# Later transposes and values in the layers' attention, and half of the differential heads' products on GpSimd

## The chip, the cores and the metric

The kernel runs on one core of a Trainium2 chip. The metric is the device time of one execution in microseconds (us), here the median of three runs. The engines are named as in the profile: PE (TensorE's matrix multiplies; PEld its weight loads), DVE (VectorE), ACT (ScalarE), POOL (GpSimd) and SP (which issues the DMAs).

## The reference, cut to what matters

The program is one transformer block with latent and sparse attention, followed by a second block of two layers. The change touches only the attention of these two layers. There, 16 heads of width 64 on 512 tokens are of three kinds: four differential heads, four block heads and eight dilated heads. Cut to the attention of a layer:

```python
# differential head: two score maps on half the width, one set of values
p = softmax(where(causal, q[c] @ k[c].T * 32 ** -0.5, NEG))   # c = 0, 1
a = p[0] - lam * p[1]
o_a = rms_norm(a @ v, g_head) * (1.0 - lam_init)
# block head and dilated head: one score map each, with their own masks
o = softmax(where(mask, q @ k.T * 64 ** -0.5, NEG)) @ v
mix = concat(o_a, o_b, o_c); x = x + mix @ w_out
```

The queries come in four blocks of 128, and a causal block j needs only the first 128 (j + 1) keys.

## The kernel before

All is in fp32. Large projections split weights and activations into a high and a low part (fp32r) and multiply three times; POOL makes the two parts of most weight slabs (`w_hi<-raw,zero_c` and `w_lo<-raw,w_hi`).

The attention of a layer is written as a list of units (`two_units`, class `Weave`). A unit has two score maps of one query block: two heads side by side ("pair"), or the two maps of one differential head ("diff"). The first 28 units are eight triples of one pair and two diffs (half 0 and half 1), with 512, 128, 384, 256 keys and the same again, and four "turn" units (numbers 6, 13, 17 and 24) that transpose operands for later. Sixteen dilated pairs follow in the same rhythm of key counts, and one "out" unit among them transposes the finished differential heads.

Every engine runs the list in its own order, in steps; step t does one part for unit t and others for units that lie a lag behind:

- PE: scores of unit t (L1845), values of unit t-5 (L1880 for pairs, L1886 for diffs), transposes of the probabilities of unit t-3 (L1862).
- DVE: mask of unit t with its row minimum (L3808), then `weigh` of unit t-1: for a pair the reciprocals of the two sums (L3817); for half 1 of a differential head the ratio of the sums (L3823, L3824) and after it the combined probabilities of both halves, `two = two * r + one` (L3829, once for each half). It also copies the second transposed tile of dilated pairs (L3837) and takes finished groups out (L3795, L3849, L3850).
- ACT: copy of the transposed tiles of unit t-3 (L2865), then the exponentials of unit t with their sums (L2857).
- POOL (`scale_pairs`): for each pair, in the order of units, waits for the reciprocals, scales both maps (L1140), and then makes one eighth of the next two weight slabs (L1104, a drain, L1108), for the eight pairs of the first 28 units; the dilated pairs have none left.

Diffs are not touched by POOL before the change. When all four differential heads are done, POOL squares them (L1123), DVE sums (L3865), ACT takes roots (L2881), DVE inverts, and POOL multiplies by gain and scale (L1127, L1132). Steps for these are fixed by numbers that count from DIFF_AT.

Buffers: four masked maps, eight probability maps, two PSUM banks for transposes, four transposed tiles.

Of the kernel before, what the change touches and what calls it, by code (L numbers as in the profile page):

```python
# [222 lines left out]
def build(nc, xT_d, slabs_d, ada_d, c_d, cols_d, rows_d, consts_d, strips_d, pos_d, cpos_d,  # L223
# [5 lines left out]
    with ctx:  # L229
# [475 lines left out]
        dilated_jobs = [job(dilated_q[h // 2], T2a[:, h // 2, :], lambda kb, h=h: z2[:, 5, kb, 64 * h:64 * h + 64],  # L705
                            None, strip2[:]) for h in range(8)]

        LAG_T, LAG_V, LAG_OUT = 3, 5, 6
        W_MASKED, W_PROBS, W_TURNED = 4, 8, 4

        class Unit:

# [15 lines left out]
        class Weave:  # L728


            def __init__(self, units):
                self.units = units
                scores = tiles = values = pairs = joins = on_act = on_dve = diffs = 0
                turned_a = 0
                self.tiles_of, self.value_of = [], []
                ends = {}
                for t, u in enumerate(units):
                    u.t, u.bank = t, 2 * (t % 2)
                    u.score, u.tile = scores, tiles
                    if u.kind == "turn":  # L740
                        turned_a += sum(len(two_turns[n][2]) for n in u.items)
                        u.turned_a = turned_a
                    if not u.jobs:
                        continue
                    scores += 2
                    values += 1
                    u.value = values
# [12 lines left out]
                for u in ends.values():  # L760
                    u.last = True
                out_order = sorted(ends, key=lambda g: ends[g].t)
                self.released = {g.index: n + 1 for n, g in enumerate(out_order)}
                self.high, self.low = {}, {}
                for t in range(len(units) + LAG_OUT):
                    if t < len(units) and units[t].kind == "out":
                        for i in units[t].items:
                            self.high[i], self.low[i] = len(self.high) + 1, len(self.low) + 1
                    for found, lag in ((self.high, LAG_V), (self.low, LAG_OUT)):
                        u = units[t - lag] if 0 <= t - lag < len(units) else None  # L770
                        if u is not None and u.last and u.group.block is not None:
# [12 lines left out]
                self.scores, self.tiles, self.values, self.pairs, self.joins = scores, tiles, values, pairs, joins  # L784
                self.on_act, self.on_dve, self.groups = on_act, on_dve, len(ends)

            def at(self, t):
# [3 lines left out]

        def sum_at(u, c):
            if u.kind == "pair":
                return 20 + 2 * (u.pair % 4) + c
            return 16 + u.join % 4 if c else 8 * (u.group.index // 2 % 2) + 4 * u.half + u.j

        def o_high(i):
# [1 line left out]
            return o_hi[:, (i + 4) % KD, :]  # L799

        def pair_inv(u):
            a = 224 + 2 * (u.pair % 4)
            return stats[:, a:a + 2]

        def w_masked(i, n):
            return ring_2[:, i % W_MASKED, 0:n]

        def w_probs(i, n):
            return ring_2[:, W_MASKED + i % W_PROBS, 0:n]

        def w_turned(v, n):
            return ring_2[:, W_MASKED + W_PROBS + v % W_TURNED, 0:n]

        HEAD = 8

# [57 lines left out]
            units.insert(DIFF_TURN, Unit("out", items=(6, 7)))  # L873
            return Weave(units)

        DILATED_AT = 28
        DIFF_AT = DILATED_AT - 1 + LAG_OUT
        DIFF_SQ, DIFF_SUM, DIFF_GAIN, DIFF_ROOT, DIFF_SCALE, DIFF_TURN = (DIFF_AT + n for n in (1, 2, 3, 3, 4, 8))

        def turn_split(src, hi, lo, n, gains=None):  # L880
            return [(lambda tt, i=i: src(tt, i), hi[:, i, :], lo[:, i, :], gains[i] if gains else None)
# [99 lines left out]
        def _(pool):  # L981
# [132 lines left out]
            def scale_pairs(n, plan, layer):  # L1114

                pieces = itertools.chain(pieces_of(n), pieces_of(n + 1))
                released = plan.groups * layer + len(nsa_jobs + mla_jobs) + plan.released[3]
                heads = O2[:].rearrange("p t (h d) -> p t h d", d=HD)
                shape = list(heads.shape)
                for u in plan.units:  # L1120
                    if u.t == DIFF_SQ:
                        pool.wait_ge(out_used, released)
                        nc.gpsimd.tensor_tensor(sq_2[:], O2[:].rearrange("p t f -> p (t f)"),  # L1123
                                                O2[:].rearrange("p t f -> p (t f)"), ALU.mult).then_inc(diff_pool, 1)
                    if u.t == DIFF_GAIN:
                        pool.wait_ge(diff_pool, 2 * layer + 1)
                        nc.gpsimd.tensor_tensor(heads, heads, row("diff", layer * HD, HD).unsqueeze(1).unsqueeze(1)  # L1127
                                                .to_broadcast(shape), ALU.mult)
                    if u.t == DIFF_SCALE + 1:
                        pool.drain()  # L1130
                        pool.wait_ge(diff_dve, 2 * layer + 2)
                        nc.gpsimd.tensor_tensor(heads, heads, stats[:, 0:16].rearrange("p (t h) -> p t h", t=TT)  # L1132
                                                .unsqueeze(3).to_broadcast(shape), ALU.mult).then_inc(diff_pool, 1)
                    if u.kind != "pair":
                        continue
                    pool.wait_ge(inverted, plan.pairs * layer + u.pair + 1)
                    inv = pair_inv(u)
# [150 lines left out]
        def _(pe):  # L1288
# [522 lines left out]
            def weave(plan, two_turned, layer, tail):  # L1811
# [37 lines left out]
                def turns(u):  # L1849
# [2 lines left out]
                        pe.wait_ge(last_taken_dve, layer + 1)  # L1852
                    for c in (0, 1) if u.kind == "pair" else (1,):
                        v = u.tile + (c if u.kind == "pair" else 0)
                        if u.kind == "diff":
                            pe.wait_ge(combined, at_.pair + u.join + 1)
                        elif c == 0:
                            pe.wait_ge(scaled_probs, at_.scaled + u.pair + 1)
                        if v >= PT_BANKS:
                            copied_before(v - PT_BANKS)  # L1860
                        for b in range(u.nb):
# [40 lines left out]
            def woven(plan):  # L1902
                at_.tile += plan.scores
                at_.value += plan.tiles
                at_.pvs += plan.values
                at_.pair += plan.joins
                at_.scaled += plan.pairs
# [998 lines left out]
        def _(dve):  # L2906
# [774 lines left out]
            for layer in range(LAYERS):  # L3681
# [131 lines left out]
                def weigh(u):  # L3813
# [5 lines left out]
                    if u.half == 0:  # L3819
# [4 lines left out]
                    then(V.scalar_tensor_tensor(out=r, in0=r, scalar=lam_c, in1=SUMS[:, a - 4:a + 1:4], op0=ALU.mult,  # L3824
                                                op1=ALU.mult))
                    for half in (0, 1):
                        score = plan.at(u.t - 1 + half).score
                        one, two = (w_probs(score + c, 128 * u.nb) for c in (0, 1))
                        V.scalar_tensor_tensor(out=two, in0=two, scalar=r[:, half:half + 1], in1=one, op0=ALU.mult,  # L3829
                                               op1=ALU.add).then_inc(combined, 1)  # L3830

                def copy(u):
                    v = u.tile + 1
# [22 lines left out]
                for t in range(len(plan.units) + LAG_OUT):  # L3856
                    u = plan.at(t)
                    if u is not None:
                        front(u)
                    u = plan.at(t - 1)  # L3860
                    if u is not None and u.jobs:
                        weigh(u)
                    if t == DIFF_SUM:
# [154 lines left out]
```

## Time and profile before

| | |
|---|---|
| median of three runs | 2188.46 us (2188.44 to 2190.65) |
| the profiled execution | 2188.03 us, of which the span is 2185.9 us |
| PE busy, whole span | 2122.7 us (97%) |
| attention of layer 0 / layer 1 in the span | from 1025 to about 1122 us / from 1666 to about 1763 us |
| PE's idle time ahead of the transposes there | 8.5 us / 8.8 us |

PE is the engine that is busy nearly all the time, so a stretch gets shorter only where PE waits or has less to do. A row of the timeline gives start, length, engine, line, operation, what was written from what, and how many instructions are merged in it; in brackets stands the idle time of that engine just ahead of the row and who ended it. PE's rows overlap by a few tenths of a microsecond, so distances are taken from start to start.

### The profile page before, as it was taken

How to read it: one execution, taken by the hardware profiler on the slowest of the kernel's cores; microseconds unless marked ns; L12 is line 12 of the kernel's file. 1: busy time of each engine (PE TensorE's matmuls, PEld its weight loads, DVE VectorE, ACT ScalarE, POOL GpSimd, SP SyncE). 2: the span in 40 equal slices, each digit the busy share in tenths (PEclk: the TensorE clock that was granted, in tenths of full speed). 3: DMA queues.
4: the chain of work that ended last, by engine and by line, in shares of the span. 5: the costliest groups of instructions: out<-in, count | busy, mean ns of one | idle time of the engine just before them, and what ended most of it. 6: DMA issues, size and time to landing. Idle time of an engine off the chain costs nothing.

```text
span 2185.9 us, 33061 instructions
## 1 busy us (share of the span) xinstructions
PE 2122.7 (97%) x12329; PEld 1788.0 (82%) x12329; DVE 1480.3 (68%) x2224; ACT 940.1 (43%) x1875; POOL 1280.7 (59%) x720
## 2 busy tenths in 40 slices
PE   6999999999999999999999999999999999999997
PEld 4788888787899988898667898888897677888886
DVE  6834877554666592897736676677996627777676
ACT  3254663112556510544744555412545725455312
POOL 5756404766477677753556644577653657454675
PEclk9999999999999999999999999999999999999998
DMA  8322103422133233221102222322321112223221
GB/s 321 154 84 97 55 25 114 175 79 94 60 115 109 105 139 135 97 97 59 39 21 77 97 97 97 116 96 78 110 84 41 39 39 97 95 80 116 97 97 58
DMA packets 32776, 206.78 MB, mean 95 GB/s; under 512 B 4080, under 2 KB 4336, under 8 KB 11632
## 3 DMA queue, kind: packets, MB, share of 16 engines
q1 hardware_dynamic: 32192, 200.27, 25.2%
q10 hardware_dynamic: 432, 4.46, 0.5%
q8 instruction: 99, 1.62, 0.3%
q14 instruction: 53, 0.43, 0.1%
HBM read 202.61 MB, written 2.10 MB: 94 GB/s over the span
## 4 chain that ended last, share of the span: by engine, by line
PE 82%; DVE 7%; issue 4%; POOL 2%; ACT 2%; DMA 2%; DVEq 1%; POOLq 1%; SPq 0%; ACTq 0%
PE PS L1293 18%; PE PS L1295 17%; PE PS L1294 17%; PE PS L1548 3%; PE PS L1549 3%; PE PS L1550 3%; PE PS L1624 2%; PE PS L1626 2%; PE PS L1625 2%; PE PS L1772 2%; PE PS L1784 2%; PE PS L1845 2%; PE PS L1862 2%; PE PS L1880 1%; PE PS L1798 1%
## 5 line engine op out<-in xcount | busy, mean ns | idle before, releaser
L997 POOL TENSOR_TENSOR w_hi<-raw,zero_c 128x512 fp32r<-128x512 f32 (+1 forms) x131 | 266.3, 2052 | 317.0 <-PE PS L1295 315.6
L1001 POOL TENSOR_TENSOR w_lo<-raw,w_hi 128x512 fp32r<-128x512 f32 (+1 forms) x131 | 347.4, 2671 | 5.5
L1293 PE MATMUL PS<-b_hi,w_hi 128*128 128x512 f32 x512 | 203.1, 397 | 0.9 <-POOL w_lo L1272 0.9
L1295 PE MATMUL PS<-b_hi,w_lo 128*128 128x512 f32 x512 | 203.0, 396 | 0.0
L1294 PE MATMUL PS<-b_lo,w_hi 128*128 128x512 f32 x512 | 203.0, 396 | 0.0
L3620 DVE TENSOR_TENSOR b_lo<-a_all,b_hi 128x512 fp32r<-128x512 f32 x44 | 162.6, 3733 | 49.3 <-ACT b_hi L2739 49.3
L1293 PE MATMUL PS<-f_hi,w_hi 128*128 128x512 f32 x448 | 177.6, 396 | 0.7 <-DVE f_lo L2921 0.7
L1295 PE MATMUL PS<-f_hi,w_lo 128*128 128x512 f32 x448 | 177.6, 396 | 0.0
L1294 PE MATMUL PS<-f_lo,w_hi 128*128 128x512 f32 x448 | 177.6, 396 | 0.0
L1140 POOL TENSOR_TENSOR ring<-ring,stats 128x512 f32<-128x512 f32 (+3 forms) x96 | 66.7, 720 | 119.1 <-DVE stats L3817 119.1
L1020 POOL TENSOR_TENSOR w_lo<-raw,w_hi 128x512 fp32r<-128x512 f32 x48 | 70.9, 1477 | 91.3 <-ACT w_hi L2731 91.3
L1293 PEld LDWEIGHTS PS<-b_hi,w_hi 128*128 128x128 f32 x512 | 96.4, 188 | 24.6 <-POOL w_lo L1272 1.1
L1295 PEld LDWEIGHTS PS<-b_hi,w_lo 128*128 128x128 f32 x512 | 96.4, 188 | 23.5
L1294 PEld LDWEIGHTS PS<-b_lo,w_hi 128*128 128x128 f32 x512 | 96.4, 188 | 23.5
L1295 PEld LDWEIGHTS PS<-f_hi,w_lo 128*128 128x128 f32 x448 | 84.4, 188 | 20.5
L1293 PEld LDWEIGHTS PS<-f_hi,w_hi 128*128 128x128 f32 x448 | 84.4, 188 | 20.1 <-issue 1.0
L1294 PEld LDWEIGHTS PS<-f_lo,w_hi 128*128 128x128 f32 x448 | 84.4, 188 | 19.1
L2739 ACT ACTIVATE b_hi<-a_all 128x512 fp32r<-128x512 f32 x44 | 25.3, 624 | 171.4 <-PE PS L1295 171.4
L1009 POOL TENSOR_TENSOR w_lo<-raw,w_hi 128x2048 fp32r<-128x2048 f32 (+1 forms) x18 | 59.1, 3295 | 62.2 <-ACT w_hi L2591 62.2
L1154 POOL TENSOR_TENSOR w_lo<-raw,w_hi 128x512 fp32r<-128x512 f32 x54 | 71.3, 1321 | 38.8 <-ACT w_hi L2629 38.8
L2857 ACT ACTIVATE ring<-ring,negmax 128x512 f32<-128x512 f32 (+3 forms) x160 | 87.8, 553 | 11.8 <-DVE negmax L3808 11.7
L3582 DVE SCALAR_TENSOR_TENSOR aux<-PS,cols,aux 128x511 f32<-128x511 f32 (+1 forms) x112 | 81.0, 741 | 14.7 <-ACT aux L2711 13.5
(588 smaller groups left out, 6826.2 us busy)
## 6 DMA issues: line engine op xcount, KB each, us to landing
raw<-slabs_dram SPq DMA_DIRECT2D x161, 1024.0 KB, 4.8
aux<-ada_dram SPq DMA_DIRECT2D x18, 512.0 KB, 5.6
ada_first<-ada_dram SPq DMA_DIRECT2D x11, 512.0 KB, 13.9
cmpw<-cmpw_dram ACTq DMA_DIRECT2D x2, 2048.0 KB, 12.9
ada_late<-ada_dram SPq DMA_DIRECT2D x8, 512.0 KB, 3.2
ada_last<-ada_dram SPq DMA_DIRECT2D x8, 512.0 KB, 5.7
xT<-xT_dram SPq DMA_DIRECT2D x1, 2048.0 KB, 9.2
out_dram<-t SPq DMA_DIRECT2D x4, 512.0 KB, 3.2
```

Source lines behind the costliest of these rows:

```text
L997: high = nc.gpsimd.tensor_tensor(w_hi[:, slot, c], raw[:, slot, c], zero[:, 0:c.stop - c.start], ALU.add)
L1001: low = nc.gpsimd.tensor_tensor(w_lo[:, slot, c], raw[:, slot, c], w_hi[:, slot, c].bitcast(f32), ALU.subtract)
L1020: return nc.gpsimd.tensor_tensor(pair_ring(w_lo, ct, n, what), pair_operand(ct, n, what), pair_ring(w_hi, ct, n, what).bitcast(f32), ALU.s ...
L1140: last = nc.gpsimd.tensor_tensor(p, p, inv[:, c:c + 1].to_broadcast([P, 128 * u.nb]), ALU.mult)
L1154: nc.gpsimd.tensor_tensor(ring_slot(w_lo, j), operand(j), ring_slot(w_hi, j).bitcast(f32), ALU.subtract).then_inc(slab_split if name == "A ...
L1293: nc.tensor.matmul(out, a_hi_, b_hi_, start=start, stop=False)
L1294: nc.tensor.matmul(out, a_hi_, b_lo_, start=False, stop=False)
L1295: return nc.tensor.matmul(out, a_lo_, b_hi_, start=False, stop=stop)
L1548: nc.tensor.matmul(out, wh[:, k, :], xh, start=first, stop=False, skip_group_check=True)
L2857: A(w_probs(i, 128 * u.nb), w_masked(i, 128 * u.nb), ACT.Exp, scale=-1.0, bias=negmax[:, i % 8:i % 8 + 1], accum_out=SUMS[:, a:a + 1]).the ...
L3582: V.scalar_tensor_tensor(out=t[:, sh:], in0=src[:, 0:SEQ - sh], scalar=cols[:, w:w + 1], in1=t[:, sh:], op0=ALU.mult, op1=ALU.add)
L3620: V.tensor_tensor(b_lo[:, f, :], a_all[:, f, :], b_hi[:, f, :].bitcast(f32), ALU.subtract).then_inc(b_low_ready, 1)
```

## The change

PE's transposes come four units behind the scores (three before), the values six (five), the outputs seven (six). DVE weighs unit t-2 in its step t (t-1 before), behind the mask of unit t. Of each differential head pair DVE now combines half 0 only; half 1 is combined by POOL in two instructions, a product with the ratio and a sum, with a drain between them. POOL takes half 1 in the order of units, so behind the pair of its triple and that pair's piece of weights. Ten probability maps are kept instead of eight (two lie in another tile), and the rings of sums and reciprocals grow from four to six. The steps of the differential norm move by up to three.

```diff
-        LAG_T, LAG_V, LAG_OUT = 3, 5, 6
-        W_MASKED, W_PROBS, W_TURNED = 4, 8, 4
+        LAG_T, LAG_V, LAG_OUT = 4, 6, 7
+        W_MASKED, W_PROBS, W_TURNED, W_SPARE = 4, 10, 4, 8
...
-        DIFF_SQ, DIFF_SUM, DIFF_GAIN, DIFF_ROOT, DIFF_SCALE, DIFF_TURN = (DIFF_AT + n for n in (1, 2, 3, 3, 4, 8))
+        DIFF_SQ, DIFF_SUM, DIFF_GAIN, DIFF_ROOT, DIFF_SCALE, DIFF_TURN = (DIFF_AT + n for n in (1, 3, 2, 4, 5, 8))
...
-                    if u.t == DIFF_SCALE + 1:
+                    if u.t == DIFF_SCALE - 1:
...
-                    if u.kind != "pair":
+                    if not u.jobs or u.kind == "diff" and u.half == 0:
                         continue
-                    pool.wait_ge(inverted, plan.pairs * layer + u.pair + 1)
+                    pool.wait_ge(inverted, plan.weighed * layer + u.weighed + 1)
+                    if u.kind == "diff":
+                        one, two = (w_probs(u.score + c, 128 * u.nb) for c in (0, 1))
+                        b = u.join % 4
+                        nc.gpsimd.tensor_tensor(two, two, ratio[:, b:b + 1].to_broadcast([P, 128 * u.nb]), ALU.mult)
+                        pool.drain()
+                        nc.gpsimd.tensor_tensor(two, two, one, ALU.add).then_inc(scaled_probs, 1)
+                        continue
...
-                        if u.kind == "diff":
-                            pe.wait_ge(combined, at_.pair + u.join + 1)
-                        elif c == 0:
-                            pe.wait_ge(scaled_probs, at_.scaled + u.pair + 1)
+                        if u.kind == "diff" and u.half == 0:
+                            pe.wait_ge(combined, at_.pair + u.join // 2 + 1)
+                        elif u.kind == "diff" or c == 0:
+                            pe.wait_ge(scaled_probs, at_.scaled + u.weighed + 1)
...
-                    for half in (0, 1):
-                        score = plan.at(u.t - 1 + half).score
-                        one, two = (w_probs(score + c, 128 * u.nb) for c in (0, 1))
-                        V.scalar_tensor_tensor(out=two, in0=two, scalar=r[:, half:half + 1], in1=one, op0=ALU.mult,
-                                               op1=ALU.add).then_inc(combined, 1)
+                    dve.drain().then_inc(inverted, 1)
+                    u = plan.at(u.t - 1)
+                    b = 16 + u.join % 4
+                    one, two = (w_probs(u.score + c, 128 * u.nb) for c in (0, 1))
+                    V.scalar_tensor_tensor(out=two, in0=two, scalar=ratio[:, b - 16:b - 15], in1=one, op0=ALU.mult,
+                                           op1=ALU.add).then_inc(combined, 1)
...
-                    u = plan.at(t - 1)
+                    u = plan.at(t - 2)
                     if u is not None and u.jobs:
                         weigh(u)
```

On POOL, at the start of a layer's attention, the order before is two scalings of a pair (ring is the tile of masked maps, probabilities and transposed tiles; stats holds reciprocals and ratios), then a piece of weights:

```order
L1140 TENSOR_TENSOR ring_133<-ring_133,stats 128x512 x2
L1104 TENSOR_TENSOR w_hi<-raw,zero_c 128x512
L1108 TENSOR_TENSOR w_lo<-raw,w_hi 128x512
L1140 TENSOR_TENSOR ring_133<-ring_133,stats 128x128 x2
L1104 TENSOR_TENSOR w_hi<-raw,zero_c 128x512
L1108 TENSOR_TENSOR w_lo<-raw,w_hi 128x512
```

Now, at the same place on POOL, with the new lines L1145 and L1147 for half 1 of a differential head:

```order
L1152 TENSOR_TENSOR ring_133<-ring_133,stats 128x512 x2
L1109 TENSOR_TENSOR w_hi<-raw,zero_c 128x512
L1113 TENSOR_TENSOR w_lo<-raw,w_hi 128x512
L1145 TENSOR_TENSOR ring_133<-ring_133,stats 128x512
L1147 TENSOR_TENSOR ring_133<-ring_133 128x512
L1152 TENSOR_TENSOR ring_133<-ring_133,stats 128x128 x2
L1109 TENSOR_TENSOR w_hi<-raw,zero_c 128x512
L1113 TENSOR_TENSOR w_lo<-raw,w_hi 128x512
L1145 TENSOR_TENSOR ring_133<-ring_133,stats 128x128
L1147 TENSOR_TENSOR ring_133<-ring_133 128x128
```

So two instructions stand behind each piece of weights, and the next pair stands behind them.

On PE, at the same start (aux and T hold the operands of the scores, consts the identity for transposes, z the values), the order before is:

```order
L1845 MATMUL PS<-aux,z_129 128x512 x2
L1845 MATMUL PS<-aux,T_131 128x512 x4
L1845 MATMUL PS<-aux,z_129 128x128 x2
L1862 MATMUL PS<-consts,ring_133 128x128 x8
L1845 MATMUL PS<-aux,T_131 128x128 x2
L1862 MATMUL PS<-consts,ring_133 128x128 x4
L1845 MATMUL PS<-aux,T_131 128x128 x2
L1880 MATMUL PS<-ring_133,z_129 64x128 x8
L1862 MATMUL PS<-consts,ring_133 128x128 x4
L1840 MATMUL PS<-consts,z_129 128x128 x8
```

Now, on PE at the same place:

```order
L1857 MATMUL PS<-aux,z_129 128x512 x2
L1857 MATMUL PS<-aux,T_131 128x512 x4
L1857 MATMUL PS<-aux,z_129 128x128 x2
L1857 MATMUL PS<-aux,T_131 128x128 x2
L1874 MATMUL PS<-consts,ring_133 128x128 x8
L1857 MATMUL PS<-aux,T_131 128x128 x2
L1874 MATMUL PS<-consts,ring_133 128x128 x4
L1852 MATMUL PS<-consts,z_129 128x128 x8
L1892 MATMUL PS<-ring_133,z_129 64x128 x8
L1874 MATMUL PS<-consts,ring_133 128x128 x4
```

The scores of one more diff (128 keys) stand ahead of the first transposes, and the turn unit (L1840, now L1852) ahead of the third.

## Rows read from the trace of the kernel before

**Rows 1.** The page: busy time and share of each engine over the span.

```profile
PE 2122.7 (97%) x12329; PEld 1788.0 (82%) x12329; DVE 1480.3 (68%) x2224; ACT 940.1 (43%) x1875; POOL 1280.7 (59%) x720
```

**Rows 2.** Stretch of layer 0's first 28 units: busy time by engine, PEclk, DMA.

```profile
1025.00:1078.00 53.00, 48.93 (x332) 34.01 (x332) 37.78 (x136) 41.22 (x127) 27.15 (x30) 1.00 0.06 21
```

**Rows 3.** PE's waits in layer 0's attention: us in total, times, longest.

```profile
PE PS L1862 <- DVE ring L3829: 3.1, 4, 0.9
PE PS L1862 <- DVE ring L3837: 2.9, 3, 1.4
PE PS L1862 <- POOL ring L1140: 1.3, 1, 1.3
PE PS L1862 <- ACT ring L2865: 1.2, 2, 0.9
```

**Rows 4.** Layer 1's attention, PE's transposes: busy, mean ns, idle before, releasers.

```profile
L1862 PE MATMUL PS<-consts,ring 128*128 128x128 f32 x156 | 25.5, 283 | 8.8 <-DVE ring L3829 3.5 <-DVE ring L3837 2.9 <-POOL ring L1140 1.2
```

**Rows 5.** Timeline of POOL just behind layer 0's attention.

```profile
1134.56 3.60 POOL L997 TENSOR_TENSOR w_hi<-raw,zero_c 128x2048 fp32r<-128x2048 f32 x1 [12.83 <-PE PS L1295]
```

**Rows 6.** Groups of DVE in layer 0's attention with waits on ACT and POOL.

```profile
L3823 DVE RECIPROCAL stats<-rowsum 128x2 f32<-128x2 f32 x8 | 1.3, 164 | 7.1 <-ACT ring L2857 7.1
L3865 DVE TENSOR_REDUCE stats<-sq 128x16 f32<-128x1024 f32 x1 | 1.2, 1220 | 1.6 <-POOL sq L1123 1.6
```

**Rows 7.** Timeline of POOL in layer 0's attention: scalings of pairs, a piece of weights.

```profile
1029.54 2.04 POOL L1140 TENSOR_TENSOR ring<-ring,stats 128x512 f32<-128x512 f32 x2 [26.68 <-DVE stats L3817]
1031.54 1.04 POOL L1104 TENSOR_TENSOR w_hi<-raw,zero_c 128x512 fp32r<-128x512 f32 x1
1032.73 1.83 POOL L1108 TENSOR_TENSOR w_lo<-raw,w_hi 128x512 fp32r<-128x512 f32 x1
...
1042.18 1.61 POOL L1140 TENSOR_TENSOR ring<-ring,stats 128x384 f32<-128x384 f32 x2 [3.34 <-DVE stats L3817]
...
1044.93 1.27 POOL L1108 TENSOR_TENSOR w_lo<-raw,w_hi 128x512 fp32r<-128x512 f32 x1
```

**Rows 8.** Groups of POOL with two different full inputs, over the whole span.

```profile
L1020 POOL TENSOR_TENSOR w_lo<-raw,w_hi 128x512 fp32r<-128x512 f32 x48 | 70.9, 1477 | 91.3 <-ACT w_hi L2731 91.3
...
L1194 POOL TENSOR_TENSOR q_m<-m_rope 128x512 f32<-128x512 f32 x1 | 1.3, 1277 | 0.1
```

**Rows 9.** Timeline of DVE in layer 0's attention: ratios and combined probabilities.

```profile
1032.20 0.39 DVE L3824 SCALAR_TENSOR_TENSOR stats<-stats,small,rowsum 128x2 f32<-128x2 f32 x1
1032.67 2.43 DVE L3829 SCALAR_TENSOR_TENSOR ring<-ring,stats 128x512 f32<-128x512 f32 x2
...
1045.19 1.03 DVE L3824 SCALAR_TENSOR_TENSOR stats<-stats,small,rowsum 128x2 f32<-128x2 f32 x1
1046.30 1.15 DVE L3829 SCALAR_TENSOR_TENSOR ring<-ring,stats 128x384 f32<-128x384 f32 x2
...
1060.85 1.41 DVE L3829 SCALAR_TENSOR_TENSOR ring<-ring,stats 128x512 f32<-128x512 f32 x2
```

**Rows 10.** Timeline of PE: scores of three triples end, half 1 is transposed.

```profile
1029.93 0.49 PE L1845 MATMUL PS<-aux,z 64*128 64x128 f32 x4
...
1035.53 0.66 PE L1862 MATMUL PS<-consts,ring 128*128 128x128 f32 x4
1036.03 1.04 PE L1840 MATMUL PS<-consts,z 128*128 128x128 f32 x8
...
1041.35 0.44 PE L1880 MATMUL PS<-ring,z 128*64 128x128 f32 x4
...
1043.17 0.33 PE L1886 MATMUL PS<-z,ring 128*128 128x64 f32 x2
...
1049.12 0.55 PE L1862 MATMUL PS<-consts,ring 128*128 128x128 f32 x3
...
1057.93 0.55 PE L1886 MATMUL PS<-z,ring 128*128 128x64 f32 x4
...
1064.02 0.66 PE L1862 MATMUL PS<-consts,ring 128*128 128x128 f32 x4
```

More of the change, by code:

```diff
@@ L732, in __init__ @@
                 self.units = units
-                scores = tiles = values = pairs = joins = on_act = on_dve = diffs = 0
+                scores = tiles = values = pairs = joins = on_act = on_dve = weighed = 0
                 turned_a = 0
@@ L746, in __init__ @@
                     values += 1
+                    if u.kind == "pair" or u.half == 1:
+                        u.weighed, weighed = weighed, weighed + 1
                     u.value = values
@@ L783, in __init__ @@
                         self.copies.append((True, a))
-                self.scores, self.tiles, self.values, self.pairs, self.joins = scores, tiles, values, pairs, joins
+                self.scores, self.tiles, self.values, self.weighed, self.joins = scores, tiles, values, weighed, joins
                 self.on_act, self.on_dve, self.groups = on_act, on_dve, len(ends)
@@ L793, in sum_at @@
             if u.kind == "pair":
-                return 20 + 2 * (u.pair % 4) + c
+                return 20 + 2 * (u.pair % 6) + c
             return 16 + u.join % 4 if c else 8 * (u.group.index // 2 % 2) + 4 * u.half + u.j
@@ L801, in pair_inv @@
         def pair_inv(u):
-            a = 224 + 2 * (u.pair % 4)
+            a = 224 + 2 * (u.pair % 6)
             return stats[:, a:a + 2]
@@ L808, in w_probs @@
         def w_probs(i, n):
-            return ring_2[:, W_MASKED + i % W_PROBS, 0:n]
+            slot = i % W_PROBS
+            if slot < W_SPARE:
+                return ring_2[:, W_MASKED + slot, 0:n]
+            return T2[:, (4 if i < FIRST_SCORES else 8) + slot - W_SPARE, 0:n]
         def w_turned(v, n):
-            return ring_2[:, W_MASKED + W_PROBS + v % W_TURNED, 0:n]
+            return ring_2[:, W_MASKED + W_SPARE + v % W_TURNED, 0:n]
         HEAD = 8
@@ L874, in two_units @@
             return Weave(units)
-        DILATED_AT = 28
+        DILATED_AT, FIRST_SCORES = 28, 48
         DIFF_AT = DILATED_AT - 1 + LAG_OUT
-        DIFF_SQ, DIFF_SUM, DIFF_GAIN, DIFF_ROOT, DIFF_SCALE, DIFF_TURN = (DIFF_AT + n for n in (1, 2, 3, 3, 4, 8))
+        DIFF_SQ, DIFF_SUM, DIFF_GAIN, DIFF_ROOT, DIFF_SCALE, DIFF_TURN = (DIFF_AT + n for n in (1, 3, 2, 4, 5, 8))
         def turn_split(src, hi, lo, n, gains=None):
@@ L1905, in woven @@
                 at_.pvs += plan.values
-                at_.pair += plan.joins
-                at_.scaled += plan.pairs
+                at_.pair += plan.joins // 2
+                at_.scaled += plan.weighed
                 at_.map += plan.groups
@@ L3823, in weigh @@
                     then(V.reciprocal(r, SUMS[:, b:b + 2]))
-                    then(V.scalar_tensor_tensor(out=r, in0=r, scalar=lam_c, in1=SUMS[:, a - 4:a + 1:4], op0=ALU.mult,
-                                                op1=ALU.mult))
-                    for half in (0, 1):
-                        score = plan.at(u.t - 1 + half).score
-                        one, two = (w_probs(score + c, 128 * u.nb) for c in (0, 1))
-                        V.scalar_tensor_tensor(out=two, in0=two, scalar=r[:, half:half + 1], in1=one, op0=ALU.mult,
-                                               op1=ALU.add).then_inc(combined, 1)
+                    V.scalar_tensor_tensor(out=r, in0=r, scalar=lam_c, in1=SUMS[:, a - 4:a + 1:4], op0=ALU.mult,
+                                           op1=ALU.mult)
+                    dve.drain().then_inc(inverted, 1)
[4 more added lines that the diff above has]
+                                           op1=ALU.add).then_inc(combined, 1)
                 def copy(u):
```

## The prediction

> **What bounds the kernel now.** I read the page first: PE is busy 97% of the span, every other engine at most 68% [rows 1]. Then the busy time of the stretch that is changed: in the 53 us of a layer's first 28 units PE works 48.9, ACT 41.2, DVE 37.8 and POOL 27.2 us, at the full granted clock [rows 2]. So PE bounds there too, but with about 4 us of holes. Third, who ends the holes: in the attention of layer 0 PE waits 8.5 us, of which 3.1 in four pieces are for DVE's combined probabilities (L3829), 2.9 in three for DVE's copies (L3837), 1.3 for the first scaling of POOL and 1.2 for ACT [rows 3]; layer 1 has 8.8 us [rows 4]. These 17.3 us are all that can be won, 0.8% of the time. What is won or lost there reaches the end: right behind the attention POOL sits idle 12.8 us until PE lets go of a slab, so nothing else is waiting to become late [rows 5].
>
> Last, why DVE is late: it waits 7.1 us for ACT's exponentials ahead of its ratios and 1.6 us for POOL's squares [rows 6]. The first goes with the change, since the weighing comes one mask later.
>
> **The part that is removed.** DVE loses eight L3829 a layer, 0.58 to 0.70 us each for 384 and 512 keys where nothing disturbs them (1.15 and 1.41 for two) [rows 9], and its wait for the exponentials. PE's transposes of half 0 come one unit of PE later. I take all four waits on L3829 as gone: 3.1 and 3.5 us [rows 3, 4].
>
> **The part that is added: half 1 goes through POOL.** POOL works in order, and half 1 of a triple stands behind the pair of the triple and the pair's piece of weights. I add this chain up from where PE ends the scores of half 1 (which lets DVE weigh the pair) to where PE can transpose half 1. For 512 keys: 0.83 until the scaling starts (1041.35 to 1042.18) [rows 7, 10], two scalings 2.04, w_hi 1.04, the drain 0.15 (1032.58 to 1032.73), w_lo 1.27 [rows 7], the product 1.04 (as one scaling), a drain 0.15, the sum 1.28 (two different inputs) [rows 8], a semaphore 0.15 (taken like the drain). That is 7.95 us. To it comes DVE's combining of half 0, 0.70, since it runs when POOL wants its piece and the two don't run beside each other: L3824, an instruction of two elements, lasts until w_hi ends at 1032.58, and w_lo, 1.27 where it is undisturbed, takes 1.83 where L3829 starts just ahead of it [rows 7, 9]. Chain: 8.65 us. For 384 keys: 0.83 + 1.61 + 1.04 + 0.15 + 0.58 + 1.27 + 0.80 + 0.15 + 0.96 (three quarters of 1.28) + 0.15 = 7.54 us.
>
> The Trainium skill, "SBUF — State Buffer", section "Who interferes with whom", says the same of a DVE instruction with two SBUF inputs against a GpSimd one that reads SBUF: one of them holds the shared port for its whole length. The trace agrees (1.83 for 1.27). Its page "Perfetto Trace Analysis", section "Optimizing Scalar/DVE Operations", warns that moving work between these two engines might not help for that reason; by it the gain of this change would be nothing or less.
>
> Against the chain stands what PE has to do in between, its old waits taken out and one step added. First triple, 512 keys: from 1029.93 to 1035.53 are 5.60, less 1.5 of waits (1.3 and the short one of ACT's two, 1.2 less 0.9) [rows 3], plus the turn unit that now comes ahead, 0.9 of its 1.04 (the rest lies under its neighbour): 5.0. Second 512: 1057.93 to 1064.02 is 6.1, less one average wait of 0.8, plus 1.4 for the added step: 6.7. 384 keys: 1043.17 to 1049.12 is 5.95, less 0.9, plus 1.4 (turn unit 0.9, values of a short pair 0.4, a transpose): 6.45, all from [rows 10]; the second 384 triple is taken alike. New waits: 8.65 less 5.0 is 3.7; 8.65 less 6.7 is 1.95; 7.54 less 6.45 is 1.1, twice. Sum 7.9 us a layer. For 256 and 128 keys the chain is shorter and the next triple's scores are long: no wait.
>
> Before, the same places had 1.5 and 3.1 (layer 1: 1.4 and 3.5). So layer 0 loses 7.9 - 4.6 = 3.3 us, layer 1 3.0.
>
> Bounds for what the trace doesn't show: if DVE's combining doesn't hold POOL up and the sum costs only the product's rate, the chains are 7.7 and 6.8, the waits 4.45, and the diff stretch gains 0.15 and 0.45. If w_lo always takes 1.83 and the sum 1.48 [rows 8], the chains are 9.4 and 8.25, the waits 10.75: 6.2 and 5.9 lost. I take the middle, which is made of the nearest rows.
>
> **The rest.** The first transposes wait 1.3 already; the pair is weighed one mask later there and PE has one diff's scores more. That is inside the 3.7. The sum of squares is called for two steps later, but POOL squares one unit later and behind a pair of 384 keys (1.61) where it was 128; DVE still waits for it, about as long as the 1.6 of [rows 6]. I count nothing, between 1.5 won (two of the three L3837 waits) and 0.7 lost a layer. The third and longest L3837 wait, 1.4, is behind the "out" unit; the unit that follows is now 384 keys instead of 128, some 0.4 more of scores to cover it: 0.8 won in both layers. The deeper pipeline drains into the projection, whose first products stand between the last steps on PE: nothing. Ten probability maps and longer rings take a wait from nobody, since ACT's idle time is ended by others. SP's queue is untouched, and the weight pieces have time, as the 12.8 us show.
>
> **Sum.** 3.3 + 3.0 - 0.8 = 5.5 us. The profiled execution took 2188.03 (span 2185.9 and 2.1 around it), so 2193.5; the median shown is 0.43 above it: 2194.0 us.
>
> **The rivals.**
> - Half 1 is early enough. The chain is at its low bound, because POOL's piece often starts before DVE wants the port. For it: two of the three pairs of L3829 in [rows 9] run undisturbed. Against it: 0.39 and 1.03 for the tiny L3824. Time: -0.15 - 0.45 - 0.8 = -1.4: 2187.1.
> - Faster: DVE, freed of eight products and the wait for ACT, runs ahead by a step and POOL starts each triple 1.1 to 1.95 us earlier, the point from which its chain hides. Then all L3829 waits go (-6.6), the two shorter L3837 waits (-3.0) and 0.8 behind "out"; only the start stays (3.7 - 1.5 twice, +4.4): -6.0, 2182.5. Against it: DVE can't weigh the pair before the mask of half 1, which needs PE's scores, so it can't be earlier than the 0.83.
> - Slower still: POOL, with some 12 us more in 53 (two halves of each length, at about 2.3, 1.8, 1.2 and 0.6), carries its lateness into the next triple, so that the four triples of 128 and 256 keys wait 1 us each: 2 x 4 x 1.0 on top, 2202. Against it: POOL was idle half of the stretch.
>
> **How the numbers follow.** Forecast 0.55, its own range 2187 to 2200; early enough 0.18; faster 0.19; slower still 0.08. A measurement can tell about 0.2%, 4.4 us, from no change. Above 2192.84 lie 0.36 of the forecast and the last rival: 0.44. Below 2184.08 lie most of the third and a little of the second: 0.19. Between: 0.37. The range for 8 in 10 reaches from 2182, the faster rival, to 2200, the forecast's upper bound.
>
> **What would show it.** Right: PE's transposes wait on POOL's sum (L1147) in the 512 and 384 triples, 3 to 4 us at the start of each layer, 1 to 2 us in three later places; the waits on DVE's combining are gone; DVE no longer waits for ACT ahead of its ratios; w_lo or the product is stretched where half 0 is combined. Wrong: no wait of PE on the sum behind the first triple, or waits on DVE's combining as before, or a gain in the dilated units above 2 us a layer.

## The result and the profile after

The changed kernel takes 2193.20 us (median of 12 runs, 2191.89 to 2196.14), the kernel before, on the same chip, 2189.99 (12 runs, 2188.44 to 2191.02): ratio 1.0017, 95% interval 1.0009 to 1.0025. It is slower, as forecast, and the forecast of 2194.0 is 0.8 off. That flatters it: the forecast added 5.5 us to the 2188.46 of the kernel before, and over the 2189.99 measured here the change costs 3.2. And the profile shows that the sum stands on a wrong step.

The profiled execution took 2193.17 (span 2191.4, 5.5 more than before). By the time of PE's first scores of a layer and its last products of values (L1880, now L1892), layer 0's attention took 102.04 before and 104.11 after, layer 1's 102.32 and 105.16, what lies between them 538.9 and 540.0, all behind them 417.4 and 417.0. The instructions of the last two stretches are the same, and the seven other kernels below have 539.4 to 541.0 between the attentions, so I take the 1.1 there as noise. In these two executions the attentions are 2.1 and 2.8 us longer. That the spans differ by the forecast's 5.5 is chance: about 1.9 of it is the clock (below), which no term of the forecast has.

Lines have moved by about 12: POOL's scaling of pairs is L1152, its new product L1145 and new sum L1147, its pieces L1109 and L1113; PE's scores L1857, its transposes L1874; DVE's mask L3820, its ratio L3835 and L3836, its combining of half 0 L3842, its copies L3850; ACT's copies L2877.

The page after, line of engines; then the stretch of layer 0's first 28 units, which answers to [rows 2] (columns: stretch, its length, then busy us of PE, PEld, DVE, ACT, POOL, the granted clock, DMA):

```profile
PE 2126.8 (97%) x12329; PEld 1791.8 (82%) x12329; DVE 1475.4 (67%) x2208; ACT 939.9 (43%) x1875; POOL 1306.4 (60%) x752
```

```profile
1025.00:1078.00 53.00, 47.82 (x306) 33.56 (x307) 32.75 (x122) 38.95 (x121) 34.78 (x39) 0.97 0.06 21
```

DVE works 5.0 us less there and POOL 7.6 more, but PE has fewer instructions done in the same 53 us (306 for 332), so the list stands at another place at its end. Over the whole span, with both layers done, DVE lost 4.9 and POOL gained 25.7. And PE's clock is no longer 1.00.

PE's waits in layer 0's attention after, in us, times, longest. They answer to [rows 3]:

```profile
PE PS L1874 <- DVE ring L3842: 3.1, 2, 2.1
PE PS L1874 <- DVE ring L3850: 2.0, 2, 1.0
PE PS L1874 <- POOL ring L1152: 1.8, 1, 1.8
PE PS L1874 <- DVE T L3842: 0.9, 1, 0.9
PE PS L1874 <- ACT ring L2877: 0.6, 1, 0.6
PE PS L1857 <- ACT T2a L2857: 0.2, 1, 0.2
```

8.6 us for 8.5. The waits on DVE's combining are still there: 3.1 + 0.9 for half 0 alone (`T` is where the two new probability maps lie), where both halves had 3.1. A wait on POOL's sum stands only once, at the start of layer 1. Of that layer's PE rows with a wait, the four that concern the diffs (start, length, and in brackets the wait before it):

```profile
1682.07 0.66 PE L1874 MATMUL PS<-consts,ring 128*128 128x128 f32 x4 [0.98 <-POOL ring L1147]
...
1693.62 0.55 PE L1874 MATMUL PS<-consts,ring 128*128 128x128 f32 x3 [1.01 <-DVE ring L3842]
...
1710.02 1.11 PE L1874 MATMUL PS<-consts,ring 128*128 128x128 f32 x4 [2.10 <-DVE ring L3842]
...
1725.02 0.55 PE L1874 MATMUL PS<-consts,T 128*128 128x128 f32 x3 [0.92 <-DVE T L3842]
```

Why half 0 is late shows on DVE and POOL side by side. DVE after, half 0 of a triple of 384 keys and of the second of 512:

```profile
1048.15 1.68 DVE L3842 SCALAR_TENSOR_TENSOR ring<-ring,stats 128x384 f32<-128x384 f32 x1
...
1064.65 1.57 DVE L3842 SCALAR_TENSOR_TENSOR ring<-ring,stats 128x512 f32<-128x512 f32 x1
```

POOL after, second triple of 512 keys:

```profile
1064.64 1.04 POOL L1145 TENSOR_TENSOR T<-T,stats 128x512 f32<-128x512 f32 x1
1065.82 1.54 POOL L1147 TENSOR_TENSOR T<-T 128x512 f32<-128x512 f32 x1
```

One signal lets POOL's product and DVE's combining go, and they start some 10 ns apart. The product takes 1.04 as elsewhere, the combining 1.57 for the 0.70 of [rows 9]: here it is DVE that waits for the port, and PE stands for 2.10 us. The 1.68 of 384 keys stands beside a piece of weights instead (w_lo from 1048.14, 1.27).

The clock is the other new thing. Layer 0's windows behind the first wait, and the PE rows in them:

```profile
1034.00:1036.00 2.00, 2.00 (x12) 2.00 (x11) 1.01 (x6) 1.74 (x7) 2.00 (x2) 0.50 0.00 0
1036.00:1038.00 2.00, 2.00 (x19) 1.67 (x19) 0.00 (x0) 1.06 (x5) 1.86 (x3) 0.66 0.03 8
```

```profile
1032.94 1.06 PE L1874 MATMUL PS<-consts,ring 128*128 128x128 f32 x8 [1.80 <-POOL ring L1152]
1033.84 0.98 PE L1857 MATMUL PS<-aux,T 128*128 128x128 f32 x4
1034.61 1.06 PE L1874 MATMUL PS<-consts,ring 128*128 128x128 f32 x4
1035.46 1.92 PE L1852 MATMUL PS<-consts,z 128*128 128x128 f32 x8
```

The granted clock is 0.50, which is 1.2 GHz, for some 3 us. The turn unit takes 1.92 there and 1.04 in [rows 10]. This slow stretch covers layer 0's wait on POOL's sum: PE comes so late to half 1 (1038.33) that the sum is there (1037.88). Layer 1 has its own slow stretch behind the 2.10 (1710 to 1713 at 0.50). Before, both attentions ran at 1.00 throughout.

Three smaller rows. DVE's ratios no longer wait for ACT, its sum of squares waits 2.0 for POOL (1.6 in [rows 6]), and POOL behind the attention is idle as in [rows 5]:

```profile
L3835 DVE RECIPROCAL stats<-rowsum 128x2 f32<-128x2 f32 x8 | 1.3, 160 | 0.0
L3878 DVE TENSOR_REDUCE stats<-sq 128x16 f32<-128x1024 f32 x1 | 1.2, 1220 | 2.0 <-POOL sq L1128 2.0
```

```profile
1136.82 3.60 POOL L1002 TENSOR_TENSOR w_hi<-raw,zero_c 128x2048 fp32r<-128x2048 f32 x1 [12.90 <-PE PS L1307]
```

### The profile page after: what moved, and what is told of

Same layout as the page of the kernel before. It is cut to its first block, busy times and chain, and to the rows that moved or that the text cites. A ratio compares the mean times of both kernels' runs of the same rounds, so it can differ in the third digit from the quotient of the medians.

```text
span 2191.4 us, 33083 instructions
## 1 busy us (share of the span) xinstructions
PE 2126.8 (97%) x12329; PEld 1791.8 (82%) x12329; DVE 1475.4 (67%) x2208; ACT 939.9 (43%) x1875; POOL 1306.4 (60%) x752
## 4 chain that ended last, share of the span: by engine, by line
PE 80%; DVE 8%; issue 4%; POOL 3%; DMA 2%; ACT 1%; DVEq 1%; POOLq 1%; SPq 0%; ACTq 0%
PE PS L1305 17%; PE PS L1307 17%; PE PS L1306 17%; PE PS L1560 3%; PE PS L1561 3%; PE PS L1562 3%; PE PS L1636 2%; PE PS L1637 2%; PE PS L1638 2%; PE PS L1784 2%; PE PS L1796 2%; PE PS L1857 2%; PE PS L1874 1%; DMA raw<-slabs_dram 1%; PE PS L1810 1%
## 5 line engine op out<-in xcount | busy, mean ns | idle before, releaser
L1152 POOL TENSOR_TENSOR ring<-ring,stats 128x512 f32<-128x512 f32 (+3 forms) x76 | 53.4, 726 | 84.7 <-DVE stats L3829 84.6
L1306 PEld LDWEIGHTS PS<-f_lo,w_hi 128*128 128x128 f32 x448 | 84.4, 188 | 19.1
L1066 POOL TENSOR_TENSOR w_lo<-raw,w_hi 128x1024 fp32r<-128x1024 f32 x24 | 65.5, 2741 | 30.0 <-DVE aux L3730 20.3
```

Of the source, the lines that this page charges most:

```text
L1306: nc.tensor.matmul(out, a_hi_, b_lo_, start=False, stop=False)
```

## The theories and the experiments

The question: why did one unit of PE more in front of the transposes not free them of DVE?

- **Distance.** The transposes went from 3 to 4 units behind the scores, and the weighing from 1 to 2 behind the mask. PE's scores release the mask, DVE weighs behind the mask: the slack is the difference of the two numbers, and that stayed 2. The kernel can win only where the difference grows.
- **Port.** The distance is good, but POOL's product and pieces block DVE's combining.
- **Chain.** As predicted: half 1's way through POOL sets the pace.
- **Lags.** The longer pipeline costs by itself.

Each kernel ran 5 to 11 times beside the kernel before, 1 to 4 in one session and 6 to 8 in another, in which before took 2189.90 and 2189.42 us; the ratios go by these. PE's waits are the sum of its single waits in the profiled execution. The number 5 is not used.

| kernel | median us | ratio to before, 95% interval | PE's waits, layer 0 / 1 | length of attention 0 / 1 |
|---|---|---|---|---|
| before | 2189.99 | | 8.5 / 8.8 | 102.04 / 102.32 |
| after | 2193.20 | 1.0017 (1.0009 to 1.0025) | 8.6 / 9.6 | 104.11 / 105.16 |
| 1 DVE both | 2188.56 | 0.9995 (0.9987 to 1.0004) | 7.7 / 7.4 | 101.75 / 103.21 |
| 2 POOL, old distances | 2200.94 | 1.0050 (1.0037 to 1.0063) | 12.4 / 12.3 | 105.68 / 108.73 |
| 3 half 0 first | 2191.71 | 1.0009 (1.0000 to 1.0017) | 9.2 / 8.9 | 103.33 / 103.33 |
| 4 piece behind | 2199.48 | 1.0044 (1.0031 to 1.0057) | 9.6 / 9.5 | 105.54 / 105.55 |
| 6 DVE both, weighed near | 2181.84 | 0.9966 (0.9952 to 0.9979) | 4.1 / 4.1 | 98.55 / 98.41 |
| 7 after, weighed near | 2181.03 | 0.9962 (0.9949 to 0.9976) | 3.9 / 3.9 | 98.13 / 98.06 |
| 8 = 7 and 3 | 2179.57 | 0.9957 (0.9943 to 0.9970) | 3.2 / 3.1 | 97.72 / 97.47 |

**Experiment 1: the distances without POOL's products.**

```diff
-                    dve.drain().then_inc(inverted, 1)
-                    u = plan.at(u.t - 1)
...
+                    for half in (0, 1):
+                        score = plan.at(u.t - 1 + half).score
...
+                               op1=ALU.add).then_inc(combined, 1)
```

> The changed kernel with its new distances (turns 4, values 6, weighing two steps behind) and its new steps of the differential norm, but DVE combines both halves again, as before the change; POOL has only pairs and pieces of weights. Theory port (the time lost sits where POOL's product and DVE's combining of half 0 start together, and the distances alone are good): PE's three waits on DVE's combining (1.0, 2.1, 0.9 us a layer) and layer 1's wait on POOL's sum (1.0) go, the start (1.8) and the copies (2.0) stay, about 4.4 us of waits a layer for 8.6 and 9.6: 2193.2 - 4.2 - 5.2 = about 2184, 2182 if the two stretches at half the clock go as well. Rival distances (the longer lags cost by themselves, by a later start and a later drain): no faster than before, 2190 to 2193.

Measured 2188.56: no different from before. So the lags win nothing, against the theory of the port, and cost nothing that the time can tell, against their own. (They may cost some tenths: layer 0 waits 0.8 us less than before, 7.7 for 8.5, and is only 0.3 shorter.) Its waits in layer 0 (L3834 is the combining of both halves, L1145 the scaling, L3842 the copies):

```profile
PE PS L1867 <- DVE ring L3834: 2.2, 2, 1.2
PE PS L1867 <- DVE ring L3842: 2.0, 2, 1.0
PE PS L1867 <- POOL ring L1145: 1.8, 1, 1.8
PE PS L1867 <- DVE T L3834: 0.9, 1, 0.9
```

With no product on POOL, PE still waits 3.2 us for DVE's combining, for 3.1 before, as the theory of distance says. The port is not out of it, though: the waits of 1.01 and 0.92 stand behind a combining of 384 keys that lasts 1.72 and 1.60 beside a piece of weights, for some 0.6 alone. The 1.24 has nothing beside it. (The row merges both halves; half 0 is 1.72 of its 2.25.)

```profile
1048.79 2.25 DVE L3834 SCALAR_TENSOR_TENSOR ring<-ring,stats 128x384 f32<-128x384 f32 x2
```

```profile
1048.83 1.27 POOL L1113 TENSOR_TENSOR w_lo<-raw,w_hi 128x512 fp32r<-128x512 f32 x1
```

So this run alone doesn't part distance and pieces; experiments 6 and 7 do. The rows of a 384 triple give the slack. Before, from the end of the scores that release the last mask ahead of the ratio (L1845) to the transposes of half 0:

```profile
1043.43 0.70 PE L1845 MATMUL PS<-aux,z 64*128 64x256 f32 x4
...
1046.97 0.55 PE L1862 MATMUL PS<-consts,ring 128*128 128x128 f32 x3 [0.94 <-DVE ring L3829]
```

and in the changed kernel:

```profile
1046.09 1.08 PE L1857 MATMUL PS<-aux,T 128*128 128x256 f32 x4
...
1049.88 0.55 PE L1874 MATMUL PS<-consts,ring 128*128 128x128 f32 x3 [1.01 <-DVE ring L3842]
```

Before, 1046.97 less 1044.13 is 2.84 us, of which PE worked 1.90; after, 1049.88 less 1047.17 is 2.71, of which it worked 1.70. The cover did not grow.

**Experiment 2: POOL's products without the distances.**

```diff
-        LAG_T, LAG_V, LAG_OUT = 4, 6, 7
+        LAG_T, LAG_V, LAG_OUT = 3, 5, 6
... (and the steps of the differential norm as before)
-                    u = plan.at(t - 2)
+                    u = plan.at(t - 1)
```

> The other part alone: POOL combines half 1 in two products, at the distances of before (turns 3, values 5, weighing one step behind, old steps of the differential norm). Theory port and the chain worked out in the prediction agree on the sign: half 1 needs 8.65 us (512 keys) and 7.5 us (384) after its scores, PE's other work covers 4.1, 5.3 and 5.0, so new waits of 4.5, 3.3 and twice 2.5, 12.8 us a layer for 4.6 before: 2190 + 16 = 2206. If the clash on the port is all that matters and POOL comes in time as it did in the changed kernel, waits on POOL's sum of at most 1 us a triple: 2194 to 2198. Rival distances: POOL's products are free and the lags are what cost, 2188 to 2190.

Measured 2200.94, 11 us more than before, between the two numbers. The sign is that of the port and the chain, but not the place: the waits are DVE's half 0, and POOL's sum is nearly in time.

```profile
PE PS L1874 <- DVE ring L3842: 5.6, 4, 1.6
PE PS L1874 <- DVE ring L3850: 2.9, 3, 1.4
PE PS L1874 <- DVE T L3842: 1.5, 1, 1.5
...
PE PS L1874 <- POOL ring L1147: 0.2, 1, 0.2
```

The chain of the prediction falls here: it asked for 12.8 us of waits on the sum, and 0.2 came. Some more is hidden, because PE, held by half 0, comes later to half 1; but with its waits for half 0 in the 512 and 384 triples (1.36, 1.60, 1.47, 1.46) taken away, the sum would have held it 2.5 us in layer 0 (an estimate from the ends of the sums). What POOL costs here is the port: in the two triples of 512 and the two of 384 keys the combining of half 0 lasts 1.82, 1.57, 1.23 and 1.23 us, for 0.7 and 0.6 undisturbed [rows 9], and PE waits 7.1 us for it in layer 0, for 3.1 before.

**Experiment 3: half 0 ahead of the product.**

```diff
-                    dve.drain().then_inc(inverted, 1)
...
                                            op1=ALU.add).then_inc(combined, 1)
+                    dve.drain().then_inc(inverted, 1)
```

> The changed kernel with one signal moved: POOL is let go on half 1 after DVE has combined half 0, not before. Theory port: the combining of 512 keys beside the product falls from 1.57 to about 0.7 us, PE's 2.1 us wait for it to about 1.2, the 0.9 to about 0.5, the 1.0 beside a piece of weights stays; POOL's sum comes 0.7 to 0.9 later, which costs about 0.7 at the start of a layer: 1 to 2 us in all gained, 2191 to 2192, and another 1 to 1.5 if layer 1's stretch at half the clock goes with the 2.1 us wait. Rival chain (half 1's path through POOL sets the pace, as the prediction had it): 0.7 us later in three or four places of each layer, 2196 to 2199.

Measured 2191.71, as the theory of the port had it, though its interval overlaps that of the changed kernel. The rows are clear. DVE's combining of the second 512 keys, no longer beside the product:

```profile
1064.79 0.75 DVE L3841 SCALAR_TENSOR_TENSOR ring<-ring,stats 128x512 f32<-128x512 f32 x1
```

0.75 for 1.57, and PE's wait there is 1.24 for 2.10. But 1.24, 1.01 and 0.92 are just what the first experiment has, so 0.86 is the product's whole share of these waits. The price is a wait of 0.45 on the sum behind it, and 0.98 at the start of both layers. In all its waits are as long as the changed kernel's (18.0 for 18.2 in both layers); that its attentions are shorter goes with the clock, which is 1.00 throughout both.

**Experiment 4: the piece of weights behind half 1.**

```diff
                         nc.gpsimd.tensor_tensor(two, two, one, ALU.add).then_inc(scaled_probs, 1)
+                        next(pieces, None)
                         continue
...
                     last.then_inc(scaled_probs, 1)
-                    next(pieces, None)
```

> The changed kernel with POOL's piece of weights (w_hi, w_lo, 2.5 us) moved from behind the pair to behind half 1's sum, so that neither half 1 nor DVE's combining of half 0 stands beside or behind it. Theory port: DVE's combining meets only the product now; the waits that a piece causes (the 1.0 of 384 keys, part of the 0.9) and layer 1's 1.0 on the sum go, the 2.1 stays as long as the product goes first: about 2 us a layer gained, 2189. Rival chain: POOL's sum comes 2.6 us earlier, but PE is already held by half 0, so only the 1.0 at layer 1's start is won: 2192. If pieces beside the next pair's scaling or the next mask cost instead, above 2193.

Measured 2199.48: wrong by 10 us. The third case named in the expectation has the sign, but no price was worked out for it. The waits it was meant to take did shrink (1.01 to 0.56; 0.92 and 0.98 gone), but the pair that follows now stands behind the piece. POOL, and the two new waits of PE:

```profile
1074.68 0.40 POOL L1145 TENSOR_TENSOR ring<-ring,stats 128x128 f32<-128x128 f32 x1 [4.35 <-DVEq L3838]
...
1075.63 1.04 POOL L1109 TENSOR_TENSOR w_hi<-raw,zero_c 128x512 fp32r<-128x512 f32 x1
1076.82 1.27 POOL L1113 TENSOR_TENSOR w_lo<-raw,w_hi 128x512 fp32r<-128x512 f32 x1
1078.04 1.61 POOL L1153 TENSOR_TENSOR ring<-ring,stats 128x384 f32<-128x384 f32 x2
```

```profile
1079.71 0.87 PE L1874 MATMUL PS<-consts,ring 128*128 128x128 f32 x6 [1.15 <-POOL ring L1153]
1093.47 1.09 PE L1874 MATMUL PS<-consts,T 128*128 128x128 f32 x8 [1.34 <-POOL T L1153]
```

POOL idles 4.35 us for DVE's ratio and then does the piece when the pair is ready. In the changed kernel the same scaling starts at 1075.34. But these waits don't make 6 us more than in the changed kernel: in all PE waits 19.1 us for 18.2. The profiled execution is 3.9 longer (2197.05 for 2193.17), of which 1.8 in the attentions; 1.7 stands ahead of them, where nothing was changed. The rest may be the clock. Slow stretches followed its two waits of 1.94, too, and the mean granted clock of its five executions is 0.9926, for 0.9948 in the twelve of the changed kernel. What the piece itself costs there stays open.

**Experiment 6: the distance made larger.** The first experiment, weighed one step behind the mask; the transposes stay at 4.

```diff
-                    u = plan.at(t - 2)
+                    u = plan.at(t - 1)
```

> The first experiment (DVE combines both halves; turns 4, values 6) with the weighing back at one step behind the mask, as before the change. Theory distance (the change moved PE's turns and DVE's weighing by one step each, so DVE still has one step between the mask it stands behind and the transposes that need it; only a distance that grows takes the waits away): half 0 gets a whole unit of PE more, at least the 1.0 to 1.5 us of one unit's scores, so the waits of 1.24, 1.01 and 0.92 on the combining and the 1.8 on the first scaling go or shrink to a few tenths; left are the copies (2.0) and about 0.6 for ACT: 8.7 us of waits a layer become about 3, and 2188.6 becomes 2177 to 2180. Rival: weighing earlier brings DVE's wait for the exponentials back (7.1 us a layer before the change) and masks behind it late, which PE's transposes or scores then wait for: 2186 to 2190.

Measured 2181.84, 6.7 us under the first experiment and 7.6 under before. From the first experiment it differs in that one number, and all waits go from 7.7 and 7.4 us (not the 8.7 of the expectation) to 4.1 in each layer. The waits on the combining fall from 3.2 us a layer to 0.24, that on the scaling from 1.8 to 0.44. The rest of the expected 9 to 12 us stands in waits that were not there before the change: PE's turn unit and a score for masks, 1.2 and 0.5 (negmax is the mask's row minimum). The mask of the first stands behind the combining of half 1, which lasts 1.76 beside w_lo. So the rival had its share, small:

```profile
PE PS L1845 <- DVE negmax L3813: 1.2, 1, 1.2
...
PE PS L1850 <- DVE negmax L3813: 0.5, 1, 0.5
...
PE PS L1867 <- POOL ring L1145: 0.4, 1, 0.4
PE PS L1867 <- DVE ring L3834: 0.2, 1, 0.2
```

**Experiment 7: the changed kernel with that one number.**

```diff
-                    u = plan.at(t - 2)
+                    u = plan.at(t - 1)
```

> The changed kernel with one number moved: weighing one step behind the mask instead of two. POOL combines half 1 as in the change. Theory distance: half 0 and the chain through POOL both start a unit of PE earlier; waits on the combining (3.1 and 0.9) and the 1.8 at the start nearly go, the 1.0 on POOL's sum too: 2178 to 2182; at most 1 us a layer behind the sixth experiment, since half 0 beside the product takes 1.57 for 0.7. Rival chain (the prediction's: half 1 through POOL needs 8.65 us and sets the pace): a unit's scores (1.0 to 1.5) more of cover are not enough for 512 keys, waits of 1 to 2 us on POOL's sum appear where half 0 no longer holds PE: 2184 to 2188.

Measured 2181.03, 12.2 us under the changed kernel, by one digit of the code. No wait on POOL's sum is left, and none on half 0 but one, though the product still stretches the combining (1.58 for 512 keys, 1.23 for 384). At the start of a layer PE waits 1.36 for half 0 (0.24 in experiment 6), this time for the piece: DVE and w_lo start some 10 ns apart, and DVE takes 1.83.

```profile
1033.62 1.83 DVE L3842 SCALAR_TENSOR_TENSOR ring<-ring,stats 128x512 f32<-128x512 f32 x1
```

```profile
1033.63 1.27 POOL L1113 TENSOR_TENSOR w_lo<-raw,w_hi 128x512 fp32r<-128x512 f32 x1
```

**Experiment 8: both.** The seventh with the third's signal.

```diff
-                    u = plan.at(t - 2)
+                    u = plan.at(t - 1)
...
-                    dve.drain().then_inc(inverted, 1)
...
+                    dve.drain().then_inc(inverted, 1)
```

> The seventh experiment, with POOL let go on half 1 only after DVE has combined half 0 (as in the third). Theory distance with the port as a minor cost: half 0 is never beside the product, but has slack anyway; half 1 comes 0.7 later: no difference from the seventh within 1.5 us. Rival chain: 0.7 us later in three or four places of each layer, 4 us slower than the seventh.

Measured 2179.57, 9.9 us under before and 13.6 under the changed kernel: the fastest of all, and 1.5 from the seventh, as the theory of distance had it (the intervals of 7 and 8 overlap, so which of them is the faster is not shown; that it is faster than 6 is clearer, since its slowest run, 2180.87, is under the fastest of 6, 2181.27). Five of its six waits in layer 0, 3.0 of 3.2 us:

```profile
PE PS L1874 <- DVE ring L3850: 1.0, 1, 1.0
PE PS L1874 <- POOL ring L1147: 0.9, 1, 0.9
PE PS L1874 <- ACT ring L2877: 0.5, 1, 0.5
PE PS L1874 <- POOL ring L1152: 0.4, 1, 0.4
PE PS L1874 <- DVE ring L3841: 0.2, 1, 0.2
```

## Why the prediction was right in its number and wrong in a step

**The removed part: failed.** The step reads "PE's transposes of half 0 come one unit of PE later. I take all four waits on L3829 as gone". Three waits stayed, 4.0 us a layer. I counted PE's move and not DVE's, which is in the same diff and which the prediction itself names ("the weighing comes one mask later"). Experiments 1 and 6 show it: with PE's move and DVE's, 3.1 us of waits on the combining stay 3.2; with PE's alone they become 0.24. By the prediction's own signs of being wrong ("no wait of PE on the sum behind the first triple, or waits on DVE's combining as before") its mechanism failed.

**The added part: places and sizes right, cause wrong in three of four.** I had new waits of 3.7, 1.95, 1.1 and 1.1 on POOL's sum. Layer 1 has 1.79 + 0.98, 2.10, 1.01 and 0.92 at the same places, 6.8 for 7.9, but only the 0.98 is on the sum. The other three would have stood there for DVE's half 0 anyway (1.24, 1.01, 0.92 in experiment 1). So two errors nearly cancelled: 3.1 to 3.5 us of waits a layer taken as gone that stayed, and 4.2 us of waits on the sum (1.95 and twice 1.1) that didn't come.

**The number: luck, for the most part.** With these errors cancelled and the start 0.9 to 1.9 us cheaper than the 3.7, the change added 0.1 and 0.8 us to PE's waits, where the prediction comes to 2.9 and 2.6 (3.3 and 3.0, less 0.4 behind "out"). The profiled attentions grew by 2.1 and 2.8 all the same, in part by the clock; and the median of before was 1.5 higher than the one that the forecast starts from. Of the 5.5 forecast, 3.2 came.

**The chain.** From the start of the scaling to the end of the sum the first triple took 7.12 us (1030.76 to 1037.88). With the 0.83 ahead and the 0.15 behind, that is 8.1 for 8.65. In the other triples it hid behind half 0: without PE's waits for that, 2.10, 1.01 and 0.92, the transposes of half 1 in layer 0 would have come at 1066.24, 1051.03 and 1081.05, and the sums ended at 1067.36, 1051.65 and 1081.60 (so waits of about 1.2, 0.7 and 0.6 for the 1.95, 1.1 and 1.1, an estimate). That DVE's combining and POOL's work don't run beside each other was right, and that the combining holds POOL up was half of it: POOL's w_lo took 1.54 for 1.27 there, but the combining of 512 and 384 keys took 1.41 to 1.68 for 0.6 to 0.7.

**The rule of the Trainium skill** ("Perfetto Trace Analysis", section "Optimizing Scalar/DVE Operations": offloading between these two engines might not help, for the shared port) held at this distance: the products cost 4.6 us over experiment 1 (2193.20 less 2188.56). It did not hold where half 0 has slack and goes first: experiment 8 is 2.3 us faster than 6, in which DVE does both.

**The rest.** The wait behind "out" fell from 1.43 to 1.01, 0.4 as forecast. The two shorter copy waits and ACT's, counted as nothing, won 0.8 a layer (1.24 + 0.21 + 0.93 became 1.02 + 0.57), inside the bounds. Nothing behind the attention moved.

**The rivals.** "Early enough" saw that POOL's sum comes in time in all triples but the first, though only because PE was held by half 0. "Faster" named the waits that could go and asked that POOL start a step earlier; that is what experiment 7 does, and it wins 8.4 us for the 6.0 given there. Its reason against it ("DVE can't weigh the pair before the mask of half 1") was no limit, only the number in the diff.

**What nobody counted: the clock.** The slow stretch in layer 1 cost 1.46 us: from the transposes of half 0 to those of half 1 are 3.52 (1710.02 to 1713.54), in layer 0 at the same place 2.06. (In experiment 2, layer 1 has two and is 3.05 longer than layer 0, which has none and the same waits.) The one in layer 0 cost only 0.40, since it took the place of the 0.98 wait on the sum. Without them the change costs about 1.7 and 1.4 us in the two attentions (an estimate: 2.07 less 0.40, 2.84 less 1.46). How often they come the profiles don't tell, being one execution each. The record has the mean granted clock of every execution: 0.9948 on average in the 12 of the changed kernel, 0.9959 in the 23 of before beside experiments 1 to 4. The difference is up to 2.4 us (0.0011 of 2190, an estimate), but within the 12 the time doesn't follow the clock (2196.14 at 0.996, 2191.89 at 0.994), so the clock's share of the 3.2 stays open.

## What to carry to other kernels

In a software pipeline, count for each pair of producer and consumer the difference of their steps, before and after: moving both by one step moves the whole pipeline and buys nothing, and it took one number, not a new schedule, to turn 3 us lost into 8 won (experiment 7). Where a slower engine takes over half of a work, let the half that the bottleneck needs first run before the other engine is let go (3 beside the changed kernel and 8 beside 7 point that way, but their intervals overlap). And a sum that comes out right is no evidence for its terms; the releasers in the list of waits are.

## What the runs showed of the hardware

- Between DVE's two-input combining and POOL's product or piece one runs at its own length, and the other lasts until it is through and then takes its own, less some 0.15. Which one is not quite a matter of the first start in the record. With DVE 56 ns ahead (experiment 8, first triple: DVE at 1032.38 took 0.75) POOL's w_lo took 1.83 for 1.27. With DVE up to 40 ns ahead (14 ns in experiment 7; 40 in experiment 1, the rows at 1048.79 and 1048.83) POOL won each time. The Trainium skill, "SBUF — State Buffer", section "Who interferes with whom", states that a DVE instruction with two SBUF inputs contends with a GpSimd one that reads SBUF, and that the port is an exclusive lock; the trace agrees (1.04 and 1.57 side by side).
- The granted clock fell to 0.50 for about 3 us behind some single PE waits of 1.4 to 2.1 us, in attentions where PE is about 90% busy. It did not after others as long: the 2.10 in layer 0 of the changed kernel and the 1.80 at the start of both layers in experiment 3 were followed by 1.00. What decides between the two is not shown. The attentions of before and of 6, 7 and 8, whose longest waits are 1.43, 1.23, 1.36 and 1.01, had none; experiment 2 had one behind a wait of 1.47 and one behind 1.43.
